# High parts of the stick-breaking sums moved from the vector to the scalar engine in a one-core hybrid encoder step

## What is computed

```python
def stick_breaking(q, k, v, q_pos, k_pos):
    z = jnp.einsum('bqhd,bkhd->bhqk', q, k) * (HEAD_DIM ** -0.5)
    mask = k_pos[None, :] < q_pos[:, None]
    log_1m = jnp.where(mask, jax.nn.log_sigmoid(-z), 0.0)
    tail = lax.cumsum(log_1m, axis=log_1m.ndim - 1, reverse=True) - log_1m
    a = jnp.where(mask, jnp.exp(jax.nn.log_sigmoid(z) + tail), 0.0)
    o = jnp.einsum('bhqk,bkhd->bqhd', a, v)
    ...
def merge_ffn(x, oa, ob, gates, ...):
    g = jax.nn.sigmoid(gates.astype(jnp.float32))
    merged = g[..., :D_MODEL] * (oa @ w_proj_a) + g[..., D_MODEL:] * (ob @ w_proj_b)
    ...
```

## Time and profile before

| | us |
|---|---|
| median of 3 runs (826.5 to 828.31) | 826.74 |
| the profiled execution | 826.33 |
| its span, first to last instruction | 824.5 |
| PE busy in the span | 813.7 |
| DVE, ACT, POOL busy | 618.9, 388.1, 295.2 |

### The profile page before, as it was taken

How to read it: one execution, slowest core, us unless ns; L and a number is a source line. 1 busy time by engine, 2 the same in 40 slices (tenths; PEclk the granted TensorE clock), 3 DMA queues, 4 the chain that set the end, 5 groups by cost and what they waited for, 6 DMA issues and landing times.

```text
span 824.5 us, 15910 instructions
## 1 busy us (share of the span) xinstructions
PE 813.7 (99%) x6154; PEld 798.6 (97%) x6154; DVE 618.9 (75%) x1073; ACT 388.1 (47%) x668; POOL 295.2 (36%) x213
## 2 busy tenths in 40 slices
PE   9999999999999999999999999999999999999996
PEld 7999999999999999999999999999999999999995
DVE  4687876356879999876338988488966889488996
ACT  5657775244667758544342333233332333323532
POOL 2562222225545545344434300651035300552330
PEclk9999999999999999999999999999999999999999
DMA  9653112451112211143313113531134113412203
GB/s 285 240 165 99 52 52 66 153 166 52 53 53 87 65 51 51 51 169 125 103 55 100 52 52 104 153 102 53 51 107 147 51 51 102 147 57 78 75 2 115
DMA packets 68416, 78.16 MB, mean 95 GB/s; under 512 B 2536, under 2 KB 65040, under 8 KB 67984
## 3 DMA queue, kind: packets, MB, share of 16 engines
q1 hardware_dynamic: 68080, 76.92, 28.9%
q10 hardware_dynamic: 288, 0.60, 0.2%
HBM read 70.15 MB, written 8.93 MB: 96 GB/s over the span
## 4 chain that ended last, share of the span: by engine, by line
PE 91%; DVE 6%; issue 1%; ACT 1%; DMA 1%; DVEq 0%; SPq 0%; ACTq 0%
PE pan L1560 59%; PE pan L1775 12%; PE att L1775 11%; PE att L1713 1%; PE att L1686 1%; PE pan L1616 1%; PE att L1703 1%; PE att L1560 1%; DVE xT L1393 1%; DMA x_rows<-in_x_sample 1%; PE att L1855 1%; PE pan L1646 1%; DVE sq_sum L1492 0%; PE att L1742 0%; DVE x_out L1479 0%
## 5 line engine op out<-in xcount | busy, mean ns | idle before, releaser
L473 POOL TENSOR_TENSOR w_lo<-raw,w_hi 128x512 fp32r<-128x512 f32 x160 | 222.8, 1416 | 416.0 <-ACT w_hi L813 178.4
L1560 PE MATMUL pan<-a_hi,w_hi 128*128 128x288 f32 x624 | 134.0, 296 | 0.0
L1560 PE MATMUL pan<-a_lo,w_hi 128*128 128x288 f32 x624 | 133.4, 295 | 0.0
L1560 PE MATMUL pan<-a_hi,w_lo 128*128 128x288 f32 x624 | 132.8, 294 | 0.0
L1560 PE MATMUL pan<-h_lo,w_hi 128*128 128x288 f32 x512 | 109.5, 296 | 0.0
L1560 PE MATMUL pan<-h_hi,w_hi 128*128 128x288 f32 x512 | 109.4, 295 | 0.0
L1560 PE MATMUL pan<-h_hi,w_lo 128*128 128x288 f32 x512 | 108.8, 294 | 0.0
L1560 PEld LDWEIGHTS pan<-a_hi,w_hi 128*128 128x128 f32 x624 | 99.7, 188 | 1.0
L1560 PEld LDWEIGHTS pan<-a_hi,w_lo 128*128 128x128 f32 x624 | 100.0, 188 | 0.0
L1560 PEld LDWEIGHTS pan<-a_lo,w_hi 128*128 128x128 f32 x624 | 99.5, 188 | 0.0
L1775 PE MATMUL pan<-F_hi,w_hi 128*128 128x288 f32 x320 | 95.4, 298 | 0.6 <-DVE xT L1393 0.6
(11 more groups left out here) (279 smaller groups left out, 1750.5 us busy)
## 6 DMA issues: line engine op xcount, KB each, us to landing
raw<-in_w_in SPq DMA_DIRECT2D x34, 512.0 KB, 4.8
raw<-in_w_up SPq DMA_DIRECT2D x32, 512.0 KB, 4.5
raw<-in_w_down SPq DMA_DIRECT2D x32, 512.0 KB, 4.7
raw<-in_w_out SPq DMA_DIRECT2D x8, 512.0 KB, 4.1
x_spill<-xT SPq DMA_DIRECT2D x1, 2304.0 KB, 7.0
xT<-x_spill SPq DMA_DIRECT2D x1, 2304.0 KB, 10.4
x_rows<-in_x_prompt SPq DMA_DIRECT2D x4, 512.0 KB, 6.8
raw<-in_w_pa SPq DMA_DIRECT2D x4, 512.0 KB, 4.4
```

The lines of the kernel that those rows point to most:

```text
L473: last = nc.gpsimd.tensor_tensor(w_lo[:, slot, k:k + 4, :], raw[:, rs, k:k + 4, j * P:(j + 1) * P], w_hi[:, slot, k:k + 4, :].bitcast(F32) ...
L1560: got = nc.tensor.matmul(out[:, h, 0:HALF], w, x[:, h * HALF:(h + 1) * HALF], start=first and n == 0, stop=last and n == 2)
```

## The change

For the prompt units alone, the rounded copies of the sums (`sp_hi<-sp`) are made by ACT and no longer by DVE. ACT's `prompt_logs` takes the place of `sb_logs`: the high part of B goes ahead of A's logarithm, those of C and A behind it, each behind a wait for DVE's second addition. DVE's `prompt_sums` takes the place of `sb_sums`: the sums of C are made ahead of the low part of B, and the sums of A ahead of the low part of C. Semaphores count as before, and nothing changes for PE, POOL, the DMAs or the sample units.

```diff
+            def sum_high(u, n):
+                cs = slice(BANK[PROMPT_ORDER[n]], BANK[PROMPT_ORDER[n]] + PROMPT_W[PROMPT_ORDER[n]])
+                act.wait_ge(sp_added, u * 3 + (n + 3))
+                nc.scalar.activation(sp_hi[:, cs], sp[:, cs], ACT.Copy).then_inc(sp_hi_ready, 1)
+
+            def prompt_logs(u, out=None):
+                for n, bank in enumerate(PROMPT_ORDER):
...
+                    nc.scalar.activation(sp[:, cs], sp[:, cs], ACT.Exp).then_inc(e_ready, 1)
+                    if n:
+                        ln(u, n - 1, PROMPT_ORDER, PROMPT_W)
...
+                sum_high(u, 0)
+                ln(u, 2, PROMPT_ORDER, PROMPT_W)
+                sum_high(u, 1)
+                sum_high(u, 2)
...
                 for q in range(2):
                     u = i * 2 + (2 + q)
-                    sb_logs(u, PROMPT_ORDER, PROMPT_W)
+                    prompt_logs(u)
                     if q or not with_gates:
                         round_next(i + 5, 2 * q)
                     else:
                         sigmoids(i - 1)
                         act.preload_act_table_set("natural_log_exp_and_others")
                     sb_weights(u, PROMPT_ORDER, PROMPT_W, parts=True)
...
-            def sb_sums(u, order, wid, adds):
-                added = 0
-                for n in range(3):
-                    added = sb_add(u, n, order, wid, adds, added)
-                    sb_split(u, n, order, wid)
+            def sum_low(u, n):
...
+                dve.wait_ge(sp_hi_ready, u * 3 + (n + 1))
+                nc.vector.tensor_tensor(sp_lo[:, cs], sp[:, cs], sp_hi[:, cs].bitcast(F32), ALU.subtract).then_inc(sp_split, 1)
+
+            def prompt_sums(u, out=None):
+                sb_add(u, 0, PROMPT_ORDER, PROMPT_W, PROMPT_ADDS, 0)
...
+                sb_add(u, 1, PROMPT_ORDER, PROMPT_W, PROMPT_ADDS, 1)
+                sum_low(u, 0)
+                sb_add(u, 2, PROMPT_ORDER, PROMPT_W, PROMPT_ADDS, 2)
+                sum_low(u, 1)
+                sum_low(u, 2)
...
-                    sb_sums(u, PROMPT_ORDER, PROMPT_W, PROMPT_ADDS)
+                    prompt_sums(u)
```

More of the change, by code:

```diff
@@ L689, in _ @@
             round_at(21)
+            def sum_high(u, n):
[4 more added lines that the diff above has]
+                for n, bank in enumerate(PROMPT_ORDER):
+                    cs = slice(BANK[bank], BANK[bank] + PROMPT_W[bank])
+                    act.wait_ge(nabs_ready, u * 3 + n + 1)
+                    nc.scalar.activation(sp[:, cs], sp[:, cs], ACT.Exp).then_inc(e_ready, 1)
+                    if n:
+                        ln(u, n - 1, PROMPT_ORDER, PROMPT_W)
+                    if n == 1 and out:
+                        out()
+                sum_high(u, 0)
+                ln(u, 2, PROMPT_ORDER, PROMPT_W)
+                sum_high(u, 1)
+                sum_high(u, 2)
             def take_v_rows(n):
@@ L1154, in sb_split @@
                 nc.vector.tensor_tensor(sp_lo[:, cs], sp[:, cs], sp_hi[:, cs].bitcast(F32), ALU.subtract).then_inc(sp_split, 1)
-            def sb_sums(u, order, wid, adds):
-                added = 0
-                for n in range(3):
-                    added = sb_add(u, n, order, wid, adds, added)
-                    sb_split(u, n, order, wid)
+            def sum_low(u, n):
+                cs = slice(BANK[PROMPT_ORDER[n]], BANK[PROMPT_ORDER[n]] + PROMPT_W[PROMPT_ORDER[n]])
+                dve.wait_ge(sp_hi_ready, u * 3 + (n + 1))
+                nc.vector.tensor_tensor(sp_lo[:, cs], sp[:, cs], sp_hi[:, cs].bitcast(F32), ALU.subtract).then_inc(sp_split, 1)
+            def prompt_sums(u, out=None):
+                sb_add(u, 0, PROMPT_ORDER, PROMPT_W, PROMPT_ADDS, 0)
+                if out:
+                    out()
+                sb_add(u, 1, PROMPT_ORDER, PROMPT_W, PROMPT_ADDS, 1)
[3 more added lines that the diff above has]
+                sum_low(u, 2)
             for u in range(2):
```

## The result

The changed kernel takes 840.21 us (median of 4 executions, 835.33 to 841.77) against 827.02 us before (4 executions, 826.5 to 828.31): a ratio of 1.0147, 95% interval 1.01 to 1.0194. It is slower, as forecast, but by 13 us where 7.4 were worked out, and lies outside the range of 828.8 to 836.0. The profiled execution took 841.77 us, with a span of 840.0, which is 15.5 above the span of before.

A forecast was written before the change was run, and what follows sets the result against it. PE was taken to bound the kernel, busy 813.7 of 824.5 us. To the profiled 826.33 came +2.5 +2.5 +2.5 -0.1 = +7.4, so 833.7; with the median 0.4 higher the forecast was 834.0 us, range 828.8 to 836.0.

The forecast's parts named there:

- no slack at the last value product: Unit 4's last value product: any delay of ACT's last high part delays PE by as much.
- Part 1: Casts leaving DVE, 12.7 us for sixteen: worth nothing where DVE is in time, at most unit 7's wait.
- Rival (c): Freed 17 us of DVE bring the weights' low parts forward and remove waits: -2.8, 823.9 us; chance 0.02.
- Part 2: Unit 7, C's remainder moved behind A's sums: 0.1 of the 0.8 us wait back, bounds 0 and 0.9.
- Part 3: Units 4, 6, 8: sigmoids and table loads wait behind ACT's last copy, delaying PE 2.5 us in each.
- The low bound: Units 4, 6, 8 if no DVE operation waits for POOL: delays of 1.2, 0.5 and 0.5, sum 2.2 us.
- The sign of being wrong: Unit 4: the prediction would be wrong if A's second addition on DVE ended before 250.1.
- It neither heals nor grows there.: After units 4, 6, 8: the shift moves PE, DVE, ACT and POOL alike into the next unit, adding nothing.
- Rival (d): Low C misses tails in units 6, 8 or next logarithms run late: up to 1 us more per unit, 834.5–837; chance 0.13.
- The range: Whole kernel time: 8 in 10 between 828.8 and 836.0 us.
- The rules: DVE's stretched operations fit an exclusive port lock with POOL; the page's 2.66 us table switch does not fit the trace's 1.28.

The follow-up runs named there:

- The last experiment: Changed kernel with only B's high part on ACT in units 4, 6, 8, and POOL's key and query operations held back in units 3 to 8: 826.2 us, ratio 0.9983.
- The opposite experiment: Kernel before with copies on ACT and the new DVE order only in units 4, 6 and 8: 838.38 us beside 827.64, ratio 1.0114.

## Why the prediction was right, and where it was wrong

- **What bounds the kernel; no slack at the last value product.** Right. In unit 4 of the changed kernel ACT's last high part ends 3.0 us later in the trace (260.84 for 257.84), and PE's last value product starts 3.0 later (261.63 for 258.63).
- **Part 1, the casts.** Right where only five units were changed: no gain that can be told (ratio 0.9991, 0.9982 to 1.0001). The last experiment has a gain, of which the casts may be the source. Rival (c) counted 17 us of DVE as freed; its busy time fell by 13.7. One reading is a little off: a cast was stretched by more than the 0.97 that the prediction gives for it, from 0.36 to 1.38 us.
- **Part 2, unit 7: 0.1 of 0.8 back.** Right in mechanism and nearly in size: 0.2 where only this was changed (18.65 and 18.61 for 18.86). In the changed kernel itself the wait is not in the list, since PE ran that unit's panel at the lower clock and came later. The forecast that unit 7 would be 18.5 long did not follow from the prediction's own 0.1 (18.86 less 0.1 is 18.8), and the measured 20.66 holds the lower clock besides.
- **Part 3, 2.5 us in each of three units.** Right: 2.57, 2.45, 2.43. The chain came out term by term: C's addition was held (0.87 for 0.42), so was B's low part (1.54 for 0.56), and A's sum was not. The low bound, 1.2 + 0.5 + 0.5, was measured with POOL held back as 0.74 + 0.46 + 0.43. The sign of being wrong, A's addition ending before 250.1, was set 0.6 too late, since the copy comes behind it; it ended at 252.53. The copies took 0.53 and 0.63 for 0.49 and 0.60.
- **"It neither heals nor grows there."** This step failed. The prediction let the shift pass through units 5, 7 and 9 unchanged, and the sum had no term for them. The runs show that a stall of 2.5 us, in two or three pieces with short products between them, is followed by almost 7 us at half the clock, which costs 8.0 us for the three units behind: that is what idle matmuls in the gaps took back, with the same stalls. By periods the profiled execution is 826.33 + 7.45 + 7.55 + 0.5 = 841.8. Rival (d) was the only one above the forecast; it had up to 1 us for each unit and other mechanisms, a late tail or late logarithms, of which the profile shows none.
- **The range.** With a second term of up to 8 us, the top of 836.0 was 4 below the median. The executions differ together with the granted clock: 841.77, 841.68, 838.74 and 835.33 us at granted clocks of 0.985, 0.985, 0.993 and 0.995. The fastest of them, with a clock near that of before, lies within the range. The opposite experiment shows the same series (841.97 at 0.984 to 836.28 at 0.995). That a fall of the clock and not something beside it is what differs between executions is only argued, since one execution of each kernel has a trace.
- **The rules.** The rows bear out the lock of the Trainium skill, "SBUF — State Buffer", section "SBUF: two separate sides": with POOL's three operations away, none of DVE's operations from B's second addition to A's was stretched in unit 4. The 2.66 us that the Trainium skill, "ScalarE: Activation LUTs", section "What ACT_TABLE_LOAD costs", has for a table switch do not show here: the load took 1.28 and the next activation began 0.02 later, in the changed kernel too.

What stays open: what decides between a stall that leaves the clock and one that does not. Stalls of 1.7 us and less left it. Those of 2.2 us and more brought a fall, but it lasted from some 3 to almost 7 us, and what it cost the next unit lay between nothing and 2.9 us. No length between 1.7 and 2.2 us was tried.

## What to carry to other kernels

Before work is moved to an engine because that engine has time, look at what stands behind it in that engine's queue: an inserted instruction is cheap, its wait is not. Here a copy of 0.6 us held back 5.0 us of independent work (sigmoids and table loads) that had been hidden by nothing but its early place. Where the bound engine is PE, price a stall twice, once as time and once as the clock behind it, and test the second by filling the stall with idle matmuls. And an engine that nobody waits for can still set the time, by holding up one that is waited for.

## What the runs showed of the hardware

- After stalls in which PE was busy 3.6 of 5 us, the granted clock was 0.51 over the next 7 us (lower level), though PE was busy 6.5 of them. With the gaps filled (4.9 of 5 us) it stayed at 1.00. The unit behind such a stall was 3.0 us longer for this alone (20.68 for 17.72 in unit 5).
- In the changed kernel a low part of the sums of 384 columns, with two SBUF operands, took 0.56 us whenever POOL was idle, and 1.53 to 1.54 in the five cases where it ran against POOL's operations. The sums that read PSUM took 0.54 to 0.56 and 0.68 in all cases.
- Idle matmuls can make a kernel faster: 835.99 us with 72 of them, 841.77 without, in the profiled executions (medians 837.04 and 840.21, on two chips).
